# Expert loop of a mixture-of-experts layer: padding rows left out of the gathers, result rows stored by an indirect transfer

## The chip, the cores and the metric

The kernel runs on one core of one Trainium2 chip. The metric is the device time of one execution in microseconds (us); lower is better. The kernel before was run three times: 1900.81, 1901.49 and 1906.64 us, median 1901.49 us.

## What is computed

One inference step of a two-layer hybrid trunk for 640 tokens (128 context tokens and 512 latent tokens) of width 1024. Each layer has a mixer (three kinds of attention and a convolution, gated and summed) and then a mixture of experts, and only the latter matters here:

```python
lg = h @ moe_w_group + moe_b_group              # 4 groups
gi = argmax(lg);  gw = max(softmax(lg))
le = (h @ moe_w_expert + moe_b_expert)          # 16 experts, 4 per group
tv, ti = top_k(le[its group], 2)                # two experts per token
tw = softmax(tv) * gw
gate, up = split(h @ moe_w1[e])                 # 1024 -> 2 x 256
y += tw_e * (silu(gate) * up) @ moe_w2[e]       # 256 -> 1024
x = x + gate2 * y
```

640 tokens with two experts each make 1280 rows of work per layer. Counted with the reference on its drawn inputs, experts 0 to 15 get 97, 58, 88, 105, 82, 105, 144, 95, 59, 43, 50, 56, 64, 84, 71 and 79 rows in layer 0, and 50, 65, 63, 60, 63, 66, 46, 61, 113, 104, 86, 101, 74, 115, 103 and 110 in layer 1.

## The kernel before, in words

Everything is in fp32 in memory; a matmul is made of three fp16 passes (high times high, high times low, low times high; L428), so each weight tile that arrives is split: ScalarE writes the high part (L1617), VectorE subtracts to get the low part (L2363).

**Routing.** VectorE (L2391 to L2512) finds each token's two experts, and each row's place in a list of chunks. A chunk is 128 rows of one expert. Chunks 0 to 15 are the first 128 rows of experts 0 to 15; rows beyond 128 of an expert go to chunks from 16 on. Rows of an expert fill its chunk from row 0 up, one row per SBUF partition; what is left of the chunk is padding. `idxall` (one column per chunk, one entry per partition) holds the token number of each row, and 0 for padding, so a padding row is a copy of token 0. `sloti` holds, for each token, where its two result rows are. `route_ready` lets the loop start.

**The expert loop** runs over p*2+5 chunks; with these inputs p is 6 in both layers, which makes 17 chunks (c = 0 to 16) in each. Work per chunk:

- POOL (GpSimd, L1784 to L1789) waits until the transposes of chunk c-2 have left the buffer, copies the index column and issues an indirect DMA that gathers the 128 token rows (4 KB each) of chunk c from `h2_rows` in HBM into `xg[c % 2]`. The trace calls that tensor `h_rows`, and the buffer, which lies in a larger one, `hpart`. The first three chunks are gathered ahead of the loop (L1780 to L1782), chunk 0 into a buffer of its own.
- PE (TensorE, L1230 to L1249) computes in the order: gate/up matmuls of chunk c, k = 0 to 4 (15 matmuls), the 8 transposes of chunk c+1's rows (L1185, `turn_rows`, which counts `ht_done`), gate/up k = 5 to 7 (9 matmuls), the down matmuls of chunk c-1 (12), 2 transposes of the activations (L1208).
- ScalarE casts and copies (L1617, L1640, L1646, L1652) and copies the result out of PSUM into `ybuf[c % 2]` (L1659, `rows_back`, which counts `my_ready`); before that it waits until the store of chunk c-2 from the same buffer has landed (`y_out`, L1658).
- SP (SyncE) issues, in its own order, three 1 MB weight loads per chunk (L709: two halves of w1, and w2), each of which waits until the low part of the tile that it overwrites is made (L737, L739), and one store of 128 result rows to `y_rows` (512 KB, L745), which waits for `my_ready`. In the queue the store of a chunk stands ahead of the next weight loads.

All DMAs, whoever issues them, run on the same 16 DMA engines.

**After the loop** POOL waits until all stores have landed (L1792, L1793), copies the slot indices (L1794) and issues ten indirect gathers of result rows (L1799); ScalarE scales (L1697) and VectorE adds (L2568) them, PE turns them back (L1262), VectorE adds to x (L2577). In layer 0 VectorE first runs sixteen bias adds for the next layer (L1938).

`y_rows` was filled once with finite numbers in layer 0 (L617), long before the loop.

## Time and profile before

| | us |
|---|---|
| median of the three runs | 1901.49 |
| the profiled execution, its own time | 1910.62 |
| its span in the trace | 1908.8 |
| expert loop, layer 0 and layer 1, from the first to the last transposes | about 173 and 171 |

Busy over the span: PE 87%, VectorE 63%, ScalarE 47%, POOL 22%. The page of the profile gives busy times and groups of instructions; its other views give waits, the chain of work that ended last (each instruction followed back to what released it), a timeline of one engine, the DMA issues with their time from issue to landing, and busy times by stretch. "Idle before" is the time an engine sat still just before an instruction, with the instruction that ended it.

### The profile page before, as it was taken

Reading aid. Unit: us, or ns where it says so; the run is one execution under the profiler, and the core shown is the slowest. Engines: PE = TensorE matmul, PEld = TensorE weight load, DVE = VectorE, ACT = ScalarE, POOL = GpSimd, SP = SyncE. Lnnn points to the kernel's source line nnn. Section 1 sums busy time; section 2 is a strip of 40 time slices with the busy share of each in tenths; the row PEclk is TensorE's granted clock in tenths of the full one; section 3 lists DMA queues with packets and bytes.
Section 4 is the critical chain, followed back from the end, with each engine's and each line's share of the span. In section 5 each row is a group of like instructions: output and inputs, shape, how many; then the busy total and the mean of one; then the engine's idle time right before and its main releaser. Section 6 shows DMA issues by size and latency. Waiting matters only on the chain.

```text
span 1908.8 us, 34493 instructions
## 1 busy us (share of the span) xinstructions
PE 1657.5 (87%) x13277; PEld 1112.8 (58%) x13277; DVE 1198.3 (63%) x1900; ACT 893.7 (47%) x1468; POOL 425.7 (22%) x418
## 2 busy tenths in 40 slices
PE   6799889999989974888778998899999999388776
PEld 4478766777665542434455886677776556244336
DVE  4595455777537546877665925477773584787754
ACT  3322455666541123777533226466664211377653
POOL 0033243222241201212102324322222221111102
PEclk7899999999999986999859999999999999699995
DMA  8555235532327465999624732222223553399954
GB/s 296 181 197 171 68 132 182 183 104 73 115 104 255 157 253 190 350 380 365 241 112 144 246 125 87 77 98 73 73 73 127 197 195 120 126 362 371 373 210 166
DMA packets 191106, 350.71 MB, mean 184 GB/s; under 512 B 15477, under 2 KB 98934, under 8 KB 190710
## 3 DMA queue, kind: packets, MB, share of 16 engines
q1 hardware_dynamic: 181647, 319.58, 47.8%
q0 software_dynamic: 7776, 28.32, 4.0%
q8 instruction: 97, 1.59, 0.3%
q10 hardware_dynamic: 1543, 0.88, 0.2%
q14 instruction: 43, 0.35, 0.1%
HBM read 287.72 MB, written 61.01 MB: 183 GB/s over the span
## 4 chain that ended last, share of the span: by engine, by line
PE 65%; DVE 12%; DMA 9%; ACT 5%; issue 5%; DVEq 2%; SPq 1%; another core or an unknown queue 1%; ACTq 0%; POOL 0%; POOLq 0%
PE PS L431 38%; PE PS L438 10%; DMA wf<-in_moe_w 5%; PE PS L1055 3%; PE PS L1039 3%; DMA arena<-in_moe_w 3%; PE PS L857 2%; PE PS L813 1%; DVE arena L2363 1%; PE PS L839 1%; PE PS L823 1%; ACT arena L1439 1%; DVE hpart L1862 1%; DVE scratch L1853 1%; DMA wf<-in_w_out 1%
## 5 line engine op out<-in xcount | busy, mean ns | idle before, releaser
L1722 POOL TENSOR_TENSOR wlo<-wf,whi 128x256 f16<-128x256 f32 (+1 forms) x268 | 278.1, 1071 | 911.4 <-ACT whi L1366 911.4
L431 PE MATMUL PS<-hpart,whi 128*128 128x320 f16 x2048 | 426.5, 301 | 15.5 <-ACT arena L1439 14.5
L431 PE MATMUL PS<-hpart,wlo 128*128 128x320 f16 x1024 | 308.0, 301 | 0.0
L431 PE MATMUL PS<-whi,hpart 128*128 128x256 f16 (+2 forms) x1568 | 298.4, 291 | 5.9 <-DVE scratch L1983 3.6
L431 PEld LDWEIGHTS PS<-hpart,whi 128*128 128x128 f16 x2048 | 191.5, 98 | 104.4 <-issue 34.9
L431 PE MATMUL PS<-wlo,hpart 128*128 128x256 f16 (+2 forms) x784 | 225.7, 290 | 0.0
L431 PEld LDWEIGHTS PS<-whi,hpart 128*128 128x128 f16 x1568 | 151.9, 98 | 65.2 <-issue 24.1
L2363 DVE TENSOR_TENSOR arena<-arena 128x2048 f16<-128x2048 f32 x66 | 149.5, 2288 | 36.0 <-ACT arena L1617 35.8
L2159 DVE TENSOR_REDUCE stat<-PS 128x1 f32<-128x640 f32 (+1 forms) x160 | 110.7, 713 | 80.3 <-PE PS L1039 77.6
L1439 ACT ACTIVATE arena<-PS,pcol 128x320 f32<-128x320 f32 x128 | 67.4, 527 | 173.3 <-PE PS L431 167.9
L1617 ACT CAST arena<-arena 128x2048 f16<-128x2048 f32 x66 | 123.4, 1897 | 41.2 <-DMA arena<-in_moe_w 28.1
L1993 DVE SCALAR_TENSOR_TENSOR scratch<-scratch,cw 128x655 f32<-128x655 f32 x120 | 138.8, 1198 | 4.8 <-issue 0.4
L1529 ACT ACTIVATE scratch<-PS,stat 128x640 f32<-128x640 f32 (+1 forms) x160 | 112.9, 708 | 39.2 <-DVE stat L2159 38.3
L1366 ACT CAST whi<-wf 128x1024 f16<-128x1024 f32 (+1 forms) x84 | 109.8, 1307 | 39.7 <-PE PS L438 28.9
L431 PEld LDWEIGHTS PS<-hpart,wlo 128*128 128x128 f16 x1024 | 100.8, 98 | 40.1
L2144 DVE TENSOR_TENSOR arena<-PS,arena 128x640 f16<-128x640 f32 (+1 forms) x120 | 85.6, 713 | 49.1 <-ACT arena L1548 46.2
L2363 DVE TENSOR_TENSOR wlo<-wf,whi 128x2048 f16<-128x2048 f32 x36 | 82.3, 2291 | 43.1 <-ACT whi L1617 41.7
L431 PE MATMUL PS<-arena,hpart 128*128 128x512 f16 x384 | 96.3, 404 | 4.3 <-issue 4.1
L1548 ACT CAST arena<-PS 128x640 f16<-128x640 f32 (+1 forms) x120 | 72.8, 606 | 57.1 <-PE PS L1055 57.0
L1404 ACT COPY arena<-PS 128x256 f32<-128x256 f32 (+1 forms) x80 | 28.8, 360 | 145.0 <-PE PS L431 145.0
L431 PE MATMUL PS<-arena,scratch 128*128 128x512 f16 x408 | 93.6, 379 | 2.8 <-DVE scratch L2531 2.8
L438 PE MATMUL PS<-arena,whi 128*128 128x128 f16 (+1 forms) x512 | 91.2, 301 | 1.6 <-DVE arena L2280 1.6
(348 smaller groups left out, 2809.6 us busy)
## 6 DMA issues: line engine op xcount, KB each, us to landing
arena<-in_moe_w SPq DMA_DIRECT2D x66, 1024.0 KB, 9.9
arena<-in_w_ada SPq DMA_DIRECT2D x40, 1024.0 KB, 7.4
wf<-in_moe_w SPq DMA_DIRECT2D x36, 1024.0 KB, 9.8
wf<-in_w_gate SPq DMA_DIRECT2D x32, 1024.0 KB, 5.5
g_rows<-arena SPq DMA_DIRECT2D x128, 160.0 KB, 1.8
wf<-in_w_in SPq DMA_DIRECT2D x18, 1024.0 KB, 7.7
y_rows<-scratch SPq DMA_DIRECT2D x34, 512.0 KB, 8.8
arena<-g_rows SPq DMA_DIRECT2D x24, 640.0 KB, 5.1
```

The source lines that it names most:

```text
L431: ins = pe.matmul(out, st, mv, start=first and n == 0, stop=last and n == 2)
L438: ins = pe.matmul(pr(pair)[:, a:b], st, mv[:, a:b], start=first and n == 0, stop=last and n == 2)
L1366: return act.copy(whi[j][:, a:b] if dst is None else dst, wf[j][:, a:b])
L1439: act.activation(sg(n), bank(7, 320), ACT.Tanh, scale=0.5, bias=pcol[:, PC_BG + u % 4 * 8 + d:PC_BG + u % 4 * 8 + d + 1]).then_inc(g_ready ...
L1529: act.activation(ex[:, m % 4, 0:nk], pr(m % 2)[:, 0:nk], ACT.Exp, bias=stat[:, 0, m:m + 1], accum_out=stat[:, 1, m:m + 1]).then_inc(ex_rea ...
L1548: act.copy(pthi[:, hd % 2, 0:nk], pr(2)[:, 0:nk]).then_inc(pt_hi.sem, 1)
L1617: act.copy(mwhi[3 * j + q], mwf[3 * j + q]).then_inc(mw_hi.sem, 1)
L1722: ins = pool.tensor_tensor(lo[:, a:b], wf[j][:, a:b], hi[:, a:b], ALU.subtract)
L1993: ins = dve.scalar_tensor_tensor(out=zacc[:, c, :], in0=zpad[:, c, k:k + NZ], scalar=cw[:, c, k:k + 1], in1=zacc[:, c, :], op0=ALU.mult, o ...
L2144: dve.tensor_tensor(ptlo[:, hd % 2, 0:nk], pr(2)[:, 0:nk], pthi[:, hd % 2, 0:nk], ALU.subtract).then_inc(pt_ready.sem, 1)
L2159: dve.tensor_reduce(stat[:, 0, m:m + 1], pr(m % 2)[:, 0:nk], AX_X, ALU.max, negate=True).then_inc(mx_ready.sem, 1)
L2363: dve.tensor_tensor(mwlo[3 * j + q], mwf[3 * j + q], mwhi[3 * j + q], ALU.subtract).then_inc((mw_lo2 if q == 2 else mw_lo).sem, 1)
```

## The change

Three things are changed, all around the expert loop.

1. Padding entries of the index lists are made larger than the highest token number (except on partition 0, which stays a real token), and the gathers are told that an index beyond 639 is not transferred. The first three gathers keep indices within bounds, so that the buffers hold finite numbers. VectorE gets five small operations at the start of the routing and one more ahead of `route_ready`.
2. Result rows are no longer stored by SP but by an indirect DMA on POOL (`rows_to`), with a list `slotrow` that gives each partition its row in `y_rows`, or for padding a row beyond the bound, which is not transferred. It is made by two VectorE operations after `route_ready`. All stores leave SP's queue.
3. The order on POOL: the gather of chunk c now waits for the transposes of chunk c-1 (before: of chunk c-2), and the store of chunk c-4 is issued behind the gather of chunk c. The last four stores follow after the loop. Two tiny indirect loads at the start of the kernel take the place of the first counts of `y_out`.

```diff
--- before.py
+++ after.py
@@ -270,6 +270,7 @@
         rcol = wuf32[:, 300:340].rearrange("p (q t) -> p q t", t=5)
         ex5 = wuf32[:, 340:365].rearrange("p (t n) -> p t n", t=5)
         tie = sb("tie", [P, 4])
+        spared = sb("spared", [P, 8])
         small = wulo[:, :].bitcast(F32)
         rk = small[:, 0:266]
         iota, before = rk[:, 0:P], rk[:, P:2 * P]
@@ -279,6 +280,11 @@
         smalli = small[:, 276 + CHUNKS + 2:448].bitcast(I32)
         sloti, idxi = smalli[:, 0:10], smalli[:, 10:12]
         cexp = smalli[:, 12:12 + CHUNKS + 1]
+        idx3, slotrow = smalli[:, 38:41], smalli[:, 41:41 + CHUNKS + 2]
+        spare = small[:, 276 + CHUNKS + 2:448]
+        tokneg, padding, limit = spare[:, 68:73], spare[:, 73:74], spare[:, 74:75]
+        ownslot, padslot = spare[:, 75:75 + CHUNKS + 2], spare[:, 102:102 + CHUNKS + 2]
+        rowi = smalli[:, 129:131]
         loopf = sb("loopf", [P, 3])
         loopi = sb("loopi", [P, 3], I32)
         zero1 = sb("zero1", [P, 1], I32)
@@ -400,6 +406,7 @@
         rows_out = sig("rows_out", TILES * 16)
         route_in = sig("route_in", 16)
         route_ready = sig("route_ready", 1)
+        slots_ready = sig("slots_ready", 1)
 
         filled = sig("filled")
         base_ready = sig("base_ready", 1)
@@ -739,12 +746,6 @@
                         sp.wait_ge(mw_lo2.sem, past + (c - 1))
                     load(ds(e, 1), j, q)
 
-                def store(c, j, row):
-
-                    sp.wait_ge(my_ready.sem, past + (c + 2))
-                    sp.dma_start(t["y_rows"][ds(row, P), :] if not isinstance(row, int) else t["y_rows"][row:row + P, :],
-                                 ybuf[j]).then_inc(y_out[j].sem, 16)
-
                 sp.wait_ge(*filled(0, CHUNKS * 16))
                 load_next(2, 0, 0, 2)
                 for c in (1, 2):
@@ -757,20 +758,15 @@
                 with sp.Fori(1, p + 1) as i:
                     for n in range(2):
                         c, j = i * 2 + (1 + n), 1 - n
-                        store(i * 2 + (n - 2), n, i * (2 * P) + (n - 2) * P)
                         load_next(i * 2 + (2 + n), 1, n, i * 2 + (2 + n))
                         load_next(i * 2 + (2 + n), 2, n, i * 2 + (2 + n))
                         load_next(i * 2 + (3 + n), 0, j, i * 2 + (3 + n))
-                store(p * 2, 0, p * (2 * P))
                 load_next(p * 2 + 4, 1, 0, p * 2 + 4)
                 load_next(p * 2 + 4, 2, 0, p * 2 + 4)
-                store(p * 2 + 1, 1, p * (2 * P) + P)
                 if ahead:
                     sp.wait_ge(mw_lo.sem, past * 2 + (p * 4 + 10))
                     for u in range(2):
                         in_load(l + 1, u)
-                for c in range(3):
-                    store(p * 2 + (c + 2), c % 2, p * (2 * P) + (c + 2) * P)
                 if ahead:
                     late_load(l + 1)
 
@@ -1711,6 +1707,10 @@
 
         @block.gpsimd
         def _(pool):
+            pool.wait_ge(*set_ready(0, 5))
+            for j in range(2):
+                pool.indirect_dma_start(out=spared[:, 4 * j:4 * j + 4], out_offset=None, in_=t["k_tie"],
+                                        in_offset=bass.IndirectOffsetOnAxis(ap=zero1[:, :], axis=0)).then_inc(y_out[j].sem, 16)
             for l in range(LAYERS):
                 def low(count, j, dst=None, n=2048, piece=1024):
 
@@ -1767,7 +1767,25 @@
                 def rows_from(dst, index, done):
 
                     pool.indirect_dma_start(out=dst, out_offset=None, in_=t["h2_rows"],
-                                            in_offset=bass.IndirectOffsetOnAxis(ap=index, axis=0)).then_inc(done.sem, 16)
+                                            in_offset=bass.IndirectOffsetOnAxis(ap=index, axis=0),
+                                            bounds_check=TOK - 1, oob_is_err=False).then_inc(done.sem, 16)
+
+                def rows_to(c, j):
+
+                    pool.wait_ge(my_ready.sem, past + (c + 2))
+                    pool.tensor_tensor(rowi[:, j:j + 1], slotrow[:, ds(c, 1)], zero1[:, :], ALU.add)
+                    pool.drain()
+                    pool.indirect_dma_start(out=t["y_rows"],
+                                            out_offset=bass.IndirectOffsetOnAxis(ap=rowi[:, j:j + 1], axis=0),
+                                            in_=ybuf[j], in_offset=None,
+                                            bounds_check=CHUNKS * P - 1, oob_is_err=False).then_inc(y_out[j].sem, 16)
+
+                def rows_next(c, j):
+
+                    pool.wait_ge(ht_done.sem, past + (c - 1 + 1))
+                    pool.tensor_tensor(idxi[:, j:j + 1], idxall[:, ds(c, 1)], zero1[:, :], ALU.add)
+                    pool.drain()
+                    rows_from(xg[j], idxi[:, j:j + 1], xg_in[j])
 
                 pool.wait_ge(*rows_out(l, TILES * 16))
                 pool.tensor_tensor(zero1[:, :], zero1[:, :], zero1[:, :], ALU.add)
@@ -1777,16 +1795,21 @@
                 pool.wait_ge(*route_ready(l, 1))
                 pool.tensor_tensor(zero1[:, :], zero1[:, :], zero1[:, :], ALU.add)
                 pool.drain()
-                rows_from(xg0, idxall[:, 0:1], first_in)
-                rows_from(xg[1], idxall[:, 1:2], xg_in[1])
-                rows_from(xg[0], idxall[:, 2:3], xg_in[0])
+                rows_from(xg0, idx3[:, 0:1], first_in)
+                rows_from(xg[1], idx3[:, 1:2], xg_in[1])
+                rows_from(xg[0], idx3[:, 2:3], xg_in[0])
                 p = pairs_now(pool)
-                with pool.Fori(0, p + 1) as i:
+                pool.wait_ge(*slots_ready(l, 1))
+                pool.wait_ge(*filled(0, CHUNKS * 16))
+                rows_next(3, 1)
+                rows_next(4, 0)
+                rows_to(0, 0)
+                with pool.Fori(1, p + 1) as i:
                     for n in range(2):
-                        pool.wait_ge(ht_done.sem, past + (i * 2 + (2 + n)))
-                        pool.tensor_tensor(idxi[:, 1 - n:2 - n], idxall[:, ds(i * 2 + (3 + n), 1)], zero1[:, :], ALU.add)
-                        pool.drain()
-                        rows_from(xg[1 - n], idxi[:, 1 - n:2 - n], xg_in[1 - n])
+                        rows_next(i * 2 + (3 + n), 1 - n)
+                        rows_to(i * 2 + (n - 1), 1 - n)
+                for c in range(1, 5):
+                    rows_to(p * 2 + c, c % 2)
 
                 pool.wait_ge(hs_ready.sem, past + (p * 2 + 5))
                 pool.wait_ge(y_out[0].sem, b * 16 + (p * 16 + 64))
@@ -1813,8 +1836,6 @@
             for s in (w_lo, wo_lo, pt_ready, ot_ready, mgu_done, msilu_ready, mact_ready, at_done, at_hi, at_ready,
                       my_done, my_ready):
                 dve.nop().then_inc(s.sem, 1)
-            for s in y_out:
-                dve.nop().then_inc(s.sem, 16)
             dve.nop().then_inc(comb_ready.sem, TILES)
             dve.nop().then_inc(m_used.sem, 2)
             dve.nop().then_inc(x1_ready.sem, 2)
@@ -2388,6 +2409,13 @@
                     dve.tensor_tensor(out, out, col(7, T4), ALU.is_equal)
                     dve.drain()
 
+                dve.wait_ge(*route_in(l, 16))
+                dve.tensor_scalar(tokneg, tokid, -1024.0, None, ALU.add)
+                dve.tensor_scalar(padding, tokid[:, 0:1], 1.0, 4096.0, ALU.min, ALU.mult)
+                dve.tensor_scalar(ownslot, iota[:, 0:CHUNKS + 2], float(P), None, ALU.mult)
+                dve.drain()
+                dve.tensor_scalar(limit, padding, float(TOK - 1 - 1024), None, ALU.add)
+                dve.tensor_scalar(ownslot, ownslot, tokid[:, 0:1], None, ALU.add)
                 lg = route[:, :, 0:4]
                 oh, oh1, oh2, sel, sel2 = (rw[:, :, 16 + 4 * q:20 + 4 * q] for q in range(5))
                 first_max(lg, oh, 0)
@@ -2484,7 +2512,7 @@
                 dve.drain()
                 for ch in range(2):
                     half = chhot[:, 5 * ch:5 * ch + 5, :]
-                    ins = dve.tensor_tensor(half, half, bc(tokid.rearrange("p (n o) -> p n o", o=1), [P, 5, CH]), ALU.mult)
+                    ins = dve.tensor_tensor(half, half, bc(tokneg.rearrange("p (n o) -> p n o", o=1), [P, 5, CH]), ALU.mult)
                 ins.then_inc(place_ready.sem, 1)
                 for tile in range(3, TILES):
                     row_tile(tile)
@@ -2496,7 +2524,13 @@
                 count(loopf[:, 1:2], incl[:, 15:16], iota[:, 1:CHUNKS + 1:2], ALU.is_gt, 1, PAIRS + 1)
                 dve.tensor_scalar(loopi[:, 1:2], loopf[:, 1:2], -2.0, None, ALU.add)
                 dve.wait_ge(*list_done(l, 1))
-                dve.tensor_copy(idxall, bank(5, CHUNKS + 2)).then_inc(route_ready.sem, 1)
+                found = bank(5, CHUNKS + 2)
+                dve.tensor_scalar(idx3, found[:, 0:3], 1024.0, float(TOK - 1), ALU.add, ALU.min)
+                dve.tensor_scalar(idxall, found, limit, 1024.0, ALU.min, ALU.add).then_inc(route_ready.sem, 1)
+                dve.scalar_tensor_tensor(out=padslot, in0=found, scalar=0.0, in1=bc(padding, [P, CHUNKS + 2]),
+                                         op0=ALU.is_equal, op1=ALU.mult)
+                dve.drain()
+                dve.tensor_tensor(slotrow, padslot, ownslot, ALU.add).then_inc(slots_ready.sem, 1)
                 dve.wait_ge(*rexp_ready(l, 1))
 
                 dve.tensor_reduce(rcol[:, 3, :], ex5[:, :, 0:4], AX_X, ALU.add)
```

## Rows read from the trace of the kernel before

**Rows 1.** Busy times of two stretches, the expert loops of layers 0 and 1.

```profile
core 0: us, PE busy (x) PEld busy (x) DVE busy (x) ACT busy (x) POOL busy (x), PEclk, DMA share, GB/s
752.00:918.00 166.00, 141.68 (x683) 69.45 (x684) 130.07 (x91) 119.49 (x104) 35.66 (x28) 0.95 0.97 356
1668.00:1833.00 165.00, 141.35 (x685) 69.89 (x684) 127.60 (x90) 117.34 (x102) 29.14 (x28) 0.96 1.00 364
```

**Rows 2.** The chain that ended last, 793 to 840 us: start us, us, what.

```profile
805.33 12.91 DMA arena<-in_moe_w
...
839.01 0.37 SPq L745
```

**Rows 3.** Waits of SP's queue, 752 to 918 us: engine, line, waited for, total, times, longest.

```profile
SPq L709 <- DVE arena L2363: 91.7, 16, 11.6
SPq L745 <- ACT scratch L1659: 13.3, 9, 2.7
```

**Rows 4.** POOL by form, 752 to 918 us: line, operation, xcount, busy us, mean ns, idle before.

```profile
L1769 POOL DMA_INDIRECT hpart<-h_rows,wulo x14 | 25.6, 1832 | 17.9 <-issue 17.9
L1787 POOL TENSOR_TENSOR wulo<-wulo,zero 128x1 int32<-128x1 int32 x14 | 10.0, 715 | 105.8 <-PE PS L1185 105.8
```

**Rows 5.** Gathers of 770 to 920 us, issue to landing.

```profile
DMA to landing us min/median/max: 6.9/8.3/9.4
```

**Rows 6.** Timeline of PE around the transposes of chunks 2, 4 and 16, layer 0.

```profile
763.74 1.04 PE L1185 MATMUL PS<-ident,hpart 128*128 128x128 f32 x8
...
782.63 1.04 PE L1185 MATMUL PS<-ident,hpart 128*128 128x128 f32 x8
783.50 2.10 PE L431 MATMUL PS<-arena,hpart 128*128 128x512 f16 x9
785.44 2.75 PE L431 MATMUL PS<-arena,scratch 128*128 128x512 f16 x12
...
921.02 1.04 PE L1185 MATMUL PS<-ident,hpart 128*128 128x128 f32 x8
```

**Rows 7.** Timeline of PE, the transposes of chunks 2 and 16, layer 1.

```profile
1679.39 1.04 PE L1185 MATMUL PS<-ident,hpart 128*128 128x128 f32 x8
...
1834.64 1.04 PE L1185 MATMUL PS<-ident,hpart 128*128 128x128 f32 x8
```

**Rows 8.** Timeline of POOL at the transposes of chunk 2.

```profile
764.96 0.32 POOL L1787 TENSOR_TENSOR wulo<-wulo,zero 128x1 int32<-128x1 int32 x1 [5.73 <-PE PS L1185]
766.12 2.14 POOL L1769 DMA_INDIRECT hpart<-h_rows,wulo  x1 [0.84 <-issue]
```

**Rows 9.** VectorE's part of the routing, layer 1.

```profile
1634.04 0.18 DVE L2382 TENSOR_TENSOR wuhi<-wuhi 128x20 f32<-128x20 f32 x1
1634.30 0.18 DVE L2384 TENSOR_TENSOR wuhi<-wuhi,tie 128x20 f32<-128x20 f32 x1
```

**Rows 10.** The chain that ended last, end of the loop in layer 1.

```profile
1855.41 1.02 ACT scratch L1659
...
1856.60 2.59 DMA y_rows<-scratch
...
1860.47 0.95 POOL arena L1799
...
1861.73 5.15 DMA hpart<-y_rows,wulo
```

**Rows 11.** Timeline of VectorE after the loop in layer 0.

```profile
958.58 1.26 DVE L1938 TENSOR_TENSOR bias<-PS,arena 64x448 f32<-64x448 f32 x2 [5.87 <-remote]
...
960.34 1.28 DVE L2568 SCALAR_TENSOR_TENSOR scratch<-hpart,wuhi,arena 128x1024 f32<-128x1024 f32 x1
```

**Rows 12.** Gathers of result rows after both loops, issue to landing.

```profile
DMA to landing us min/median/max: 6.2/6.4/6.5
```

**Rows 13.** Two gathers issued at 1661.07 and 1663.24 us: the DMA issues, us to landing.

```profile
hpart<-h_rows,wulo POOLq DMA_INDIRECT x1, 8.1
...
hpart<-h_rows,wulo POOLq DMA_INDIRECT x1, 9.8
```

## The prediction

> **What bounds the kernel now.** I read the busy times of the two expert loops first [rows 1]: the 16 DMA engines are busy 0.97 and 1.00 of the time, PE 142 of 166 us. Then the timeline of PE: from the transposes of chunk 2 to those of chunk 16 it takes 921.02 - 763.74 = 157.3 us in layer 0 [rows 6] and 1834.64 - 1679.39 = 155.3 us in layer 1 [rows 7]. That is 14 chunks, so 11.23 and 11.09 us per chunk, mean 11.16. Per chunk of 11.16 us PE works 141.68/166 x 11.16 = 9.5 us, VectorE 8.7 and ScalarE 8.0 [rows 1]. So the loop is bound by the DMA engines: a chunk moves 3 MB of weights, 0.5 MB of gathered rows and 0.5 MB of result rows. The chain of waits agrees: a weight load of 12.91 us stands in it, issued behind a store in SP's queue [rows 2]. SP itself waits for buffers to come free, 91.7 us, and only 13.3 us for results [rows 3], so its queue is a small matter while the engines are full.
>
> **What is saved at most.** 17 chunks x 128 = 2176 rows are moved each way per layer, 1280 of them real: 41% are padding. Rows are 1 of 4 MB of a chunk, so 0.41 x 0.25 = 10.3% of the loop's bytes go. If all of that reached the DMA engines' time, the cycle would be 11.16 x 0.897 = 10.0 us, and PE's 9.5 us plus the stops of its in-order queue are then next. I take 10.3 us as the floor of the cycle.
>
> **The gather becomes a round trip.** The gather of chunk c was issued after the transposes of chunk c-2, and had two cycles to land. Now it is issued after the transposes of chunk c-1 and is needed by the next ones, one cycle later; PE's queue is in order, so behind those transposes stand 9 gate/up matmuls, the down matmuls and the next chunk. The cycle can't be shorter than this loop:
> - the transposes, 1.04 us [rows 6];
> - until POOL's copy starts, 764.96 - 764.78 = 0.18 us [rows 6, 8];
> - copy, drain and start of the indirect DMA: (10.0 + 17.9)/14 = 1.99 us on average [rows 4];
> - issue to landing: 6.9, 8.3 and 9.4 us (least, median, most) [rows 5].
>
> With 8.3 us that is 11.5 us, above today's 11.16; with 6.9 us it is 10.1. Today this costs nothing, since two cycles (22 us) cover it. The first intervals of the loop are shorter than the mean, (782.63 - 763.74)/2 = 9.4 us [rows 6], and those are stretched as well. How much does a gather gain from moving 41% fewer rows? Lower bound of the gain 0. Upper bound: it lands in 6.9 us, the best of today. In the quiet stretch after the loops, with DMA engines not full, full gathers still took 6.2 to 6.5 us [rows 12], so most of the time isn't the rows. Leaving out 41% of the load-dependent part, 0.41 x (8.3 - 6.3) = 0.8 us, is the most that I can argue from rows, and half of that, 0.4, is nearest to both; I take 7.9 us. Cycle: 1.04 + 0.18 + 1.99 + 7.9 = 11.1 us. 14 cycles = 155.5 us: -1.8 us in layer 0 and +0.2 in layer 1, **-1.6 us**; the bounds are 161.1 us each (+9.6 in sum) and 144.2 us each at the floor of 10.3 (-24.2).
>
> **Stores on POOL.** 34 stores leave SP, whose loads could then be issued earlier; while the DMA engines are full, that only makes them queue longer: nothing, and up to the 13.3 us of waiting per layer [rows 3] should they stand idle, which the 0.97 and 1.00 speak against. POOL gets a second copy and indirect DMA per chunk: 2 x (0.72 + 1.28 + 1.83) = 7.7 us [rows 4], below the cycle, so POOL's queue holds. Is a result buffer free in time? The store of chunk c is issued behind the gather of chunk c+4, so from the start of the transposes of chunk c+3: 1.04 + 0.18 + 1.99 + 1.83 + 1.99 = 7.0 us, and lands 8.3 us later at 15.3. The copy into the same buffer waits for the down matmuls of chunk c+2, whose end is a cycle plus the stretch from 782.63 to 788.19 [rows 6] later: 11.1 + 5.6 = 16.7 us. 1.4 us to spare; its price is nothing while that holds. What is queued behind the store on POOL is the next gather, some 7 us away.
>
> **Head of the loop.** Five small VectorE operations ahead of the first maximum, with two dependent steps of 0.26 us [rows 9] and some 0.05 to 0.1 for each of the others, and one more ahead of `route_ready`: 0.7 us per layer, **+1.4 us**. The two behind `route_ready` delay only low parts of weights. The wait for the index of the stores and for the fill of `y_rows` ended long before.
>
> **Tail.** In layer 1 the chain runs copy to `ybuf`, store, gathers [rows 10]: the copy ends at 1856.43, the store lands 2.59 us after its issue at 1856.60. The indirect store needs about 1.16 us until its issue (764.96 to 766.12) [rows 8] and then lands in 2.6 us (as SP's did) at least, in 6.5 [rows 12] at most; I take the 5.15 us after which the first pair of indirect gathers released ScalarE [rows 10]. 1.2 + 5.15 - 2.8 = +3.5, less a little since the last chunk of layer 1 is empty but for one row: **+3.2 us** (+1.0 to +4.9). In layer 0 VectorE reaches the sums only at 960.34, behind bias adds that stood still 5.87 us until 958.58 [rows 11]. What they wait for ("remote") isn't shown; it may move with the gathers or not: 0 to 3.2, **+1.6 us**.
>
> **Sum.** -1.6 + 1.4 + 3.2 + 1.6 = +4.6 us on the profiled execution of 1910.6 us, which stands 9 us above the median; so 1906.1 against 1901.5.
>
> **One rule weighed.** The DMA engines' share is a mean over 16 [rows 1], which doesn't show whether relief is even. The Trainium skill, "DMA: Bandwidth & Descriptors", section "The descriptor swizzle", says that in a 128-partition transfer each engine serves fixed partitions: engines 0 to 7 partitions 0 to 63, the others 64 to 127. By it a sum would lack the DMA relief almost wholly (rival B). No row here shows it.
>
> **Rivals.**
> - A. *The relief reaches the loop.* Gathers land in 7 us or less and the cycle falls to 10.3 us. For it: full DMA engines [rows 1] and 10.3% fewer bytes, the store's wait gone from SP. Against: 8.3 us of landing of which 6.3 remain in quiet [rows 5, 12]. -24.2 + 6.2 = -18.0: **1883.5 us**.
> - B. *Slower: the gather lands no sooner.* Padding sits at the high rows of a chunk. If a row's partition fixes its DMA engine, the half of the engines with rows 0 to 63 keeps, by the counts per expert, 986 and 983 of 1088 rows (9% less), the other half 294 and 297 (73% less). A weight load and a gather land with the slowest engine. So the landing stays 8.3 us, the cycle is 11.5: +9.6 + 6.2 = +15.8, **1917.3 us**. It decides from a landing of 8.0 us on, where the round trip passes today's cycle.
> - C. *Two indirect DMAs per chunk hold each other up.* At the start of layer 1, the third of three gathers issued close together landed in 9.8 us and the second in 8.1 [rows 13]. Were every one 9.8, the cycle would be 13.0: 182 us per loop, +52 + 6: **1960 us**. Against: gather and store are issued some 4 us apart and the next gather 7 us later.
> - D. *Rows beyond the bound are moved or cost as much all the same*: then B's time.
>
> **Chances.** Forecast (round trip near 11.1 us, between 10.9 and 11.4) 0.45; A 0.27; B and D 0.22; C 0.06. The measurement can tell about 0.3%, 5.7 us, from no change. The forecast's own range is 1901 to 1914: of its 0.45, 0.04 are faster, 0.23 within and 0.18 slower. B has 0.02 within. Faster 0.31, same 0.25, slower 0.44. Likeliest time 1906 us. The range reaches from A (1883) past B, 1883 to 1922; C is left out. Cases of both signs hold most of the chance, and the forecast lies close to the border of "no change".
>
> **What would show it.** Right: PE waits before the transposes (L1185) for the gather in most chunks, the interval from chunk 2's to chunk 16's stays near 155 us, DMA share falls to about 0.9, SP's wait for results is gone, the end of layer 1 is 3 us longer from the last copy to the first gather. Wrong: intervals of 145 us with gathers landing in 7 us (A); a DMA share near 0.9 with landings of 8 us and more and intervals above 160 (B); landings of 10 us (C); as many software packets as before plus those of the stores (D); ScalarE waiting for `y_out` at its copy.

## The result and the profile after

Eight executions, four of each kernel: 1992.99 us for the changed kernel (1987.28 to 2001.80) against 1901.29 us for the kernel before (1900.81 to 1906.64). The ratio is 1.048, with an interval of 1.0437 to 1.0523. It is slower by 92 us, where 1906 was forecast and 1922 was the end of the range. Of the runs of the experiments one (2509.77 us, of e5_count_for_drain) showed a granted clock of 0.64 where its other seven had 0.92 to 0.93, and its ratio leaves it out.

The profiled execution of the changed kernel took 1992.42 us with a span of 1990.6, that of before 1910.62 with 1908.8. The stretches of the two loops that answer to [rows 1], with the busy times of the engines in the same columns, granted clock, DMA share and GB/s last:

```profile
790.00:950.00 160.00, 116.31 (x484) 57.50 (x482) 92.95 (x63) 86.66 (x75) 32.20 (x42) 0.84 0.74 260
1720.00:1880.00 160.00, 119.13 (x504) 59.49 (x503) 98.45 (x68) 88.72 (x77) 32.93 (x42) 0.85 0.75 257
```

The DMA engines have fallen from 0.97 and 1.00 to 0.74 and 0.75, and no engine is fuller than before. PE works 116 of 160 us. So the loop is bound by a wait and not by work. Its pace, from the transposes of chunks 2 and 16 of each layer (timeline of PE, answers to [rows 6, 7]):

```profile
764.63 0.93 PE L1181 MATMUL PS<-ident,hpart 128*128 128x128 f32 x7
...
963.66 1.09 PE L1181 MATMUL PS<-ident,hpart 128*128 128x128 f32 x8 [1.58 <-DMA hpart<-h_rows,wulo]
...
1717.65 1.04 PE L1181 MATMUL PS<-ident,hpart 128*128 128x128 f32 x8
...
1918.41 1.09 PE L1181 MATMUL PS<-ident,hpart 128*128 128x128 f32 x8 [0.73 <-DMA hpart<-h_rows,wulo]
```

That is 199.0 us in layer 0 (157.3 before) and 200.8 in layer 1 (155.3 before): +41.8 and +45.5, 87.3 us in all. The rest of the kernel is 5.5 us shorter (+0.9 ahead of chunk 2 of layer 0, -4.4 between the loops, -2.0 behind the second), which gives the +81.8 us between the two profiled executions. The whole loss is in the loops. Within them a chunk takes 15.0 us over most of the way, for example from 831.63 to 846.56.

What the engines wait for, from 790 to 950 us (time in all, times, longest):

```profile
POOL hpart L1769 <- issue: 76.6, 11, 7.2
POOL y_rows L1778 <- issue: 48.3, 10, 5.3
...
PE PS L1181 <- DMA hpart<-h_rows,wulo: 41.4, 10, 7.0
...
POOL wulo L1786 <- PE PS L1181: 0.2, 1, 0.2
```

PE waits 4 us per chunk for the gathered rows (L1181). POOL waits 7.0 us ahead of each gather and 4.8 ahead of each store, 125 of 160 us, and nothing that the profile can name ends these waits ("issue"). For PE it almost never waits (0.2 us in all). So POOL, 20% busy, sets the pace. Its timeline over one chunk and a half:

```profile
826.24 1.01 POOL L1769 DMA_INDIRECT hpart<-h_rows,wulo  x1 [7.05 <-issue]
827.28 0.20 POOL L1776 TENSOR_TENSOR wulo<-wulo,zero 128x1 int32<-128x1 int32 x1
832.46 1.46 POOL L1778 DMA_INDIRECT y_rows<-scratch,wulo  x1 [4.98 <-issue]
833.95 0.20 POOL L1786 TENSOR_TENSOR wulo<-wulo,zero 128x1 int32<-128x1 int32 x1
841.24 1.01 POOL L1769 DMA_INDIRECT hpart<-h_rows,wulo  x1 [7.10 <-issue]
```

From gather to store 6.22 us, from store to the next gather 8.78: 15.0 together. Between the copy of the index, 0.2 us long, and the indirect DMA stands only the drain. The instructions of its sequencer show it (L1777 ahead of the store, L1787 ahead of the gather; shortest, median and longest in ns, 790 to 950 us), and in the second fence the one drain per chunk of the kernel before, in its loop:

```profile
L1777 POOLq DRAIN  x11: 5197/5486/6138, 796.3 to 945.8; - x11
L1787 POOLq DRAIN  x11: 5984/6805/8392, 787.1 to 938.5; - x11
```

```profile
L1788 POOLq DRAIN  x10: 345/1428/3174, 798.4 to 897.4; - x10
```

And the landings of the indirect DMAs in that stretch (median us behind their issue):

```profile
hpart<-h_rows,wulo POOLq DMA_INDIRECT x11, 5.4
y_rows<-scratch,wulo POOLq DMA_INDIRECT x10, 7.9
```

The drain behind a gather takes 5.5 us where gathers land in 5.4. The drain behind a store takes 6.8 where stores land in 7.9 and the drain begins about 1.2 us after the issue. One by one it fits too. In the chain of waits POOL's first instruction behind the drain starts at 831.69 and at 840.50; the gather of 826.24 landed 5.3 us later, at 831.5, the store of 832.46 7.9 us later, at 840.4. The same holds for each of the 20 drains from 802 to 952 us: its record ends 0.1 us behind the landing of the indirect DMA ahead of it.

The padding rows do stay out: the packets of the indirect queue moved 32.91 MB, where all rows moved both ways make 46.15 MB (e4_all_rows below).

```profile
q0 software_dynamic: 12736, 32.91, 4.5%
```

### The profile page after: what moved, and what is told of

It is laid out like the page before. It is cut to its first block, busy times and chain, and to the rows that moved or that the text cites. A ratio compares the mean times of both kernels' runs of the same rounds, so it can differ in the third digit from the quotient of the medians.

```text
span 1990.6 us, 34617 instructions
## 1 busy us (share of the span) xinstructions
PE 1692.0 (85%) x13277; PEld 1131.2 (57%) x13277; DVE 1207.3 (61%) x1916; ACT 893.3 (45%) x1468; POOL 464.9 (23%) x488
## 3 DMA queue, kind: packets, MB, share of 16 engines
q0 software_dynamic: 12736, 32.91, 4.5%
## 4 chain that ended last, share of the span: by engine, by line
PE 56%; issue 21%; DVE 8%; DMA 7%; ACT 3%; POOL 2%; POOLq 2%; DVEq 1%; SPq 0%; ACTq 0%
PE PS L438 33%; PE PS L445 8%; DMA hpart<-h_rows,wulo 4%; PE PS L1051 3%; PE PS L1035 3%; PE PS L853 2%; PE PS L809 1%; DMA wf<-in_w_out 1%; POOL hpart L1769 1%; PE PS L1181 1%; PE PS L835 1%; POOLq L1787 1%; ACT arena L1435 1%; DVE hpart L1883 1%; DVE scratch L1874 1%
## 5 line engine op out<-in xcount | busy, mean ns | idle before, releaser
L438 PE MATMUL PS<-whi,hpart 128*128 128x256 f16 (+2 forms) x1568 | 307.6, 297 | 5.9 <-DVE scratch L2004 3.6
L438 PE MATMUL PS<-wlo,hpart 128*128 128x256 f16 (+2 forms) x784 | 230.6, 297 | 0.0
L1181 PE MATMUL PS<-ident,hpart 128*128 128x128 f32 x272 | 52.1, 354 | 98.9 <-DMA hpart<-h_rows,wulo 98.9
L1362 ACT CAST whi<-wf 128x1024 f16<-128x1024 f32 (+1 forms) x84 | 109.8, 1307 | 39.8 <-DMA wf<-in_w_out 20.7
L1181 PEld LDWEIGHTS PS<-ident,hpart 128*128 128x128 f32 x272 | 41.5, 181 | 114.4 <-DMA hpart<-h_rows,wulo 113.5
L438 PE MATMUL PS<-arena,hpart 128*128 128x512 f16 x384 | 102.7, 424 | 0.3
```

Of the source, the lines that this page charges most:

```text
L438: ins = pe.matmul(out, st, mv, start=first and n == 0, stop=last and n == 2)
L1181: ins = pe.transpose(PS[:, 0, k * P:(k + 1) * P], rows[:, k * P:(k + 1) * P], ident[:, :])
L1362: return act.copy(whi[j][:, a:b] if dst is None else dst, wf[j][:, a:b])
```

## The experiments

**Theory** after this reading: the drain between the copied index and the indirect DMA stands until the indirect DMA ahead of it has landed; with two per chunk, a chunk takes two landings. **Rivals**: the indirect stores are slow whatever stands between; VectorE or a shared port holds POOL; the padding rows beyond the bound cost the time; the gather issued a cycle later costs it. The labels below are those of the kernels. Each ratio is taken against runs of the kernel before from the same batch, whose medians were 1907.20 us (experiments 1 to 3), 1894.22 (4 to 6) and 1905.40 (7 and 8), so ratios are to be compared and not times.

**1. Stores back on SP.** Both kernels keep the gathers with the bound; the stores are SP's plain ones of all 128 rows. The second also issues each gather a cycle earlier, as before.

```
 SP:    store(c, j, row) as in the kernel before, at the same places in its queue
 POOL:  - rows_to(...)                                              # both
 POOL:  - pool.wait_ge(ht_done.sem, past + (c - 1 + 1))             # second
        + pool.wait_ge(ht_done.sem, past + (c - 1))
```

> The stores go back to SP's queue as before; the gathers keep their bound and their late wait (transposes of chunk c-1). Theory 1 (POOL's queue: behind an indirect DMA, the next copy's drain stands until that DMA's descriptors are made, 6.2 us after a gather and 8.8 us after a store, 15.0 us per chunk in sum): with one indirect DMA per chunk POOL has time, the loop goes back to 11 us per chunk, total 1895 to 1920 us. Theory 2 (the late gather's round trip is what binds): stays within 30 us of 1993.

> As e1, and the gather of chunk c waits for the transposes of chunk c-2 again, as before; what is left of the change is the padding omitted from the gathers (5% of the loop's bytes) and six VectorE operations. Theory 1: 1885 to 1905 us. Against e1 it gives the price of the late wait where POOL is free: by my round trip (1.0 + 0.2 + 2.0 + landing of 5.4 to 8.3) 0 to 15 us. If DMA relief doesn't reach the slowest engine: 1900 to 1905 us.

Measured: 1913.49 us and 1902.97 us; ratios 1.0026 (0.9998 to 1.0053) and 0.9978 (0.9958 to 0.9999). With the stores off POOL the 90 us are gone. The late wait alone costs 10.5 us, the difference of the two medians (9 us by the ratios): in e1_sp_stores PE waited for the gathered rows 16.3 us in 160, in e2_sp_stores_early not at all. POOL's wait ahead of the gather is 1 us in both. The waits of e1_sp_stores, 790 to 950 us:

```profile
PE PS L1192 <- DMA hpart<-h_rows,wulo: 16.3, 11, 2.8
...
POOL hpart L1776 <- issue: 10.7, 12, 0.9
```

So the late gather is real, and a ninth of the loss in size. What is left of the change in the second kernel, above all the padding omitted from the gathers, is worth 0.2%.

**2. The padding rows moved as well.** The change with one constant different, so that padding indices stay valid.

```
-dve.tensor_scalar(padding, tokid[:, 0:1], 1.0, 4096.0, ALU.min, ALU.mult)
+dve.tensor_scalar(padding, tokid[:, 0:1], 1.0, 0.0, ALU.min, ALU.mult)
```

> The changed kernel with padding set to 0: every index is within bounds, so all 2176 rows are gathered and stored, through the same instructions. Theory 1 (making of descriptors and drain): POOL's cycle stays about 15 us or grows a little, total 1985 to 2020 us, with the DMA share up from 0.74 to about 0.85. Theory 3 (the omission itself makes the indirect DMA slow): the gaps of 5 and 7 us shrink, total below 1950 us.

Measured: 2006.14 us, ratio 1.0523 (1.0462 to 1.0584). The stops of POOL (its waits), the landings and, in the list of queues, 13 MB more:

```profile
POOL hpart L1769 <- issue: 78.2, 11, 7.4
POOL y_rows L1778 <- issue: 49.6, 10, 5.3
```

```profile
hpart<-h_rows,wulo POOLq DMA_INDIRECT x11, 5.5
y_rows<-scratch,wulo POOLq DMA_INDIRECT x10, 7.9
```

```profile
q0 software_dynamic: 12736, 46.15, 6.0%
```

A gather of all 128 rows lands in 5.5 us, one with the padding left out in 5.4; the store in 7.9 both times. The omission isn't the cause, and leaving out 41% of the rows is no help to a landing. Only where nearly all rows are left out does the landing shorten: the last gather of layer 1, one real row of 128, landed in 2.5 us in the changed kernel and in 5.1 with all rows, its store in 2.1 and 3.3; the last gather of layer 0, with 16 real rows, in 3.4 and 4.2.

**3. A count in place of the drain.** The copy of the index raises a semaphore, POOL waits for that count, and one more small operation stands between it and the indirect DMA.

```
-pool.tensor_tensor(idxi[:, j:j + 1], idxall[:, ds(c, 1)], zero1[:, :], ALU.add)
-pool.drain()
+pool.tensor_tensor(idxi[:, j:j + 1], idxall[:, ds(c, 1)], zero1[:, :], ALU.add).then_inc(copied.sem, 1)
+pool.wait_ge(copied.sem, past * 2 + (nth + 3))
+pool.tensor_tensor(smalli[:, 132:133], zero1[:, :], zero1[:, :], ALU.add)
```

The same with `rowi`, ahead of the store.

> The changed kernel, but the two index copies inside the loop are waited for by a count and not by a drain. Theory 1: the drain is what waits for the descriptors, so the gaps of 5 and 7 us ahead of the indirect DMAs go, and the loop comes down to 11 to 12 us per chunk, total 1900 to 1935 us. Theory 4 (descriptors are made one DMA after another at 6 to 8 us each, whatever the instructions do): the gaps go but landings grow to 10 us and more, and the total stays above 1970 us.

Measured: 1909.76 us, ratio 1.0013 (0.9982 to 1.0045). The order of the work, the number of indirect DMAs and their rows are those of the change. The drains of the loops are gone, with a count and a small operation in their place, and with them 83 us (89 by the ratios). Its waits, 790 to 950 us:

```profile
PE PS L1182 <- DMA hpart<-h_rows,wulo: 18.5, 9, 3.5
...
POOL y_rows L1781 <- issue: 7.8, 16, 0.5
POOL hpart L1770 <- issue: 4.7, 9, 0.5
```

POOL now stands 0.5 us ahead of each. This rules out that the indirect stores are slow as such. What is left is the late gather: PE waits 18.5 us in 160.

**4. One drain for both.** Both indices are copied, one drain, then gather and store behind each other.

```
+pool.tensor_tensor(idxi[:, j:j + 1], idxall[:, ds(c, 1)], zero1[:, :], ALU.add)
+pool.tensor_tensor(rowi[:, j:j + 1], slotrow[:, ds(c - 4, 1)], zero1[:, :], ALU.add)
+pool.drain()
+rows_from(xg[j], idxi[:, j:j + 1], xg_in[j])
+pool.indirect_dma_start(out=t["y_rows"], ...)
```

> The changed kernel with both index copies of a loop step under one drain, and gather and store issued one right behind the other. Theory 1 (a drain stands until the descriptors of the indirect DMAs before it are made, 5 to 7 us each): the drain now comes only in the next step and part of the work is done while POOL waits for PE. If gather and store need 6.2 + 8.8 us one after the other whatever stands between them, the cycle stays 15 us and the total 1990; if most of that was waiting without need, as the run with counts suggests (11.3 us per chunk), it falls to 11 to 13 us, total 1905 to 1950 us.

Measured: 1943.63 us, ratio 1.0247 (1.0201 to 1.0293), a cycle of 12.4 us. Half of the loss is gone with half of the drains. The two indirect DMAs go out 1.32 us apart (821.44 and 822.76). There is one drain per chunk, and it comes only when PE has freed the buffer (its records in ns, 790 to 950 us):

```profile
L1814 POOLq DRAIN  x12: 457/1526/7065, 791.0 to 931.7; - x12
```

Six of the twelve take 0.5 us, five 2.6 to 3.2 (there one of the two index copies itself takes 2.2 us) and one 7.1. So from the second chunk on it hardly waits for a landing, and the rest of the loss is another: POOL waits for PE (75.6 of 160 us), PE for the gather (27.8), and the round trip of the late gather is longer than in experiment 1. From the transposes at 816.56 it runs over the copies at 817.97 and the issue at 821.44, lands 9.0 us later beside a store in flight, and lets the next transposes start at 830.51, 13.95 us in all.

**5. Early gathers, with counts and with drains.** The wait of experiment 1 in the kernel of experiment 3, and in the change itself.

> Counts in place of the drains, and the gather of chunk c waits for the transposes of chunk c-2 as in the kernel before. In the run with counts and late gathers PE waited 0.9 to 3.5 us in most chunks for the gather, DMA share 0.94. If the round trip was the bound there, those waits go and the cycle comes down from 11.3 to 10.3 to 10.8 us: total 1880 to 1900 us, 0.4 to 1.2% faster than the kernel before. If DMA relief doesn't reach the slowest engine: cycle 11.1, total 1900 to 1910 us.

> The changed kernel with its drains, but gathers early (transposes of chunk c-2). Theory 1: POOL never waits for PE in the loop, so nothing changes, 1980 to 2000 us. Theory 2 (late gather): the loop falls by 2 us per chunk or more, total below 1940 us.

Measured: with counts 1897.40 us, ratio 1.0009 (0.9988 to 1.0029), so PE's waits for the gather go and the 0.4 to 1.2% expected of it don't come; with drains 1980.13 us, ratio 1.044 (1.0393 to 1.0486). With drains it matters little how early POOL may start, since its own queue is what is late (waits of e7_early_drain, 790 to 950 us):

```profile
POOL hpart L1769 <- issue: 69.1, 10, 7.2
POOL y_rows L1778 <- issue: 55.0, 11, 6.6
```

**6. Less for VectorE.** A rival was that POOL's drain stands because VectorE holds something that both use. The change with the low parts of w1 made for 256 of 2048 columns (`n` is 256 for the two tiles of w1 in the loop, 2048 elsewhere); the rest of them isn't computed.

```
-dve.tensor_tensor(mwlo[3 * j + q], mwf[3 * j + q], mwhi[3 * j + q], ALU.subtract
+dve.tensor_tensor(mwlo[3 * j + q][:, 0:n], mwf[3 * j + q][:, 0:n], mwhi[3 * j + q][:, 0:n], ALU.subtract
```

> The changed kernel, but inside the loop VectorE makes the low parts of the two w1 tiles of a chunk for 256 of 2048 columns only (the other columns keep old low parts), so that VectorE works 4 us less per chunk. If making descriptors is slowed by VectorE's work on the same memory: the gap ahead of the indirect DMA behind a store falls from 7 us towards 4, behind a gather from 5 towards 3, cycle 10 to 13 us. If descriptor making has its own pace: gaps stay 7 and 5 us and the cycle 15 us.

Measured, one execution: 1980.80 us. VectorE (third busy time) works 38 us in 110, where it was 63 in the change, and POOL stands as long:

```profile
790.00:900.00 110.00, 82.07 (x345) 40.60 (x343) 38.25 (x47) 61.77 (x54) 19.68 (x30) 0.86 0.79 274
```

```profile
POOL hpart L1769 <- issue: 70.5, 11, 7.2
POOL y_rows L1778 <- issue: 58.9, 11, 7.7
```

That rival falls.

**7. Landing or a fixed time?** The kernel before, with nothing of the change but a small operation and a drain directly behind each gather of its loop.

```
 rows_from(xg[1 - n], idxi[:, 1 - n:2 - n], xg_in[1 - n])
+pool.tensor_tensor(smalli[:, 132:133], zero1[:, :], zero1[:, :], ALU.add)
+pool.drain()
```

> The kernel before with one more small POOL operation and a drain directly behind each gather of the loop; nothing else of the change is in it. POOL has nothing to do there until the next gather, so no time is expected from it in either theory (within 5 us of before). Theory 1 (a drain stands until the indirect DMA ahead of it has landed): POOL's next instruction after that drain starts within 0.2 us of the gather's landing, 6.9 to 9.4 us behind its issue, varying with it. Theory 2 (the drain waits for something of POOL itself, such as the making of the descriptors, a fixed time): the next instruction stands at one fixed distance behind the issue, whether the gather lands in 7 or in 9 us.

Measured, one execution: 1901.67 us, beside 1905.4 for the kernel before (17 runs): the drain costs nothing where POOL has nothing to do. Four such drains in a row, each with its own length in ns, and under it the landing of the gather ahead of it (issued at 820.37, 830.04, 842.53 and 852.58):

```profile
L1791 POOLq DRAIN  x1: 7647/7647/7647, 820.2 to 820.2; - x1
...
L1791 POOLq DRAIN  x1: 9379/9379/9379, 829.9 to 829.9; - x1
...
L1791 POOLq DRAIN  x1: 7662/7662/7662, 842.3 to 842.3; - x1
...
L1791 POOLq DRAIN  x1: 8944/8944/8944, 852.4 to 852.4; - x1
```

```profile
hpart<-h_rows,wulo POOLq DMA_INDIRECT x1, 7.4
...
hpart<-h_rows,wulo POOLq DMA_INDIRECT x1, 9.1
...
hpart<-h_rows,wulo POOLq DMA_INDIRECT x1, 7.4
...
hpart<-h_rows,wulo POOLq DMA_INDIRECT x1, 8.7
```

The drains end at 827.8, 839.3, 850.0 and 861.3; the gathers landed at 827.8, 839.1, 849.9 and 861.3. The drain follows the landing to 0.2 us, at 7.4 us as at 9.1, so it isn't a fixed time of POOL's. The making of the descriptors doesn't take so long either: without a drain between, indirect DMAs go out 1.26 us apart [rows 10].

**8. What the omission is worth when POOL is out of the way.** The kernel of experiment 5 with counts, and with all rows moved as in experiment 2.

> The kernel of e6 (counts in place of the drains, early gathers) with the padding indices left at a valid row, so that all 128 rows of every chunk are moved each way: 10.3% more bytes in the loop than e6, nothing else changed. Theory 1 (with POOL out of the way the omission is what makes e6's cycle 10.56 and 10.77 us against 11.16 of before): the cycle goes back to 11.1 to 11.3 us in both layers, the time is 10 to 17 us above e6, that is 1.005 to 1.010 of the kernel before. Theory 2 (the shorter cycle of e6 comes from the loads that no longer stand behind stores in SP's queue, and the omitted rows give little, as in e2): the cycle stays within 0.15 us of e6's, the time within 4 us of it.

Measured: 1900.50 us, ratio 0.9979 (0.9950 to 1.0009), beside e6_count_early's 1.0009 (0.9988 to 1.0029). From the transposes of chunk 2 to those of chunk 16 it takes 149.1 and 147.8 us with all rows, 147.0 and 149.2 without the padding. The same stretch of both (DMA share and GB/s are the last two), all rows first:

```profile
790.00:900.00 110.00, 96.70 (x471) 47.67 (x472) 88.21 (x63) 83.53 (x73) 68.78 (x61) 0.97 1.02 387
```

```profile
790.00:900.00 110.00, 94.86 (x465) 47.17 (x466) 87.75 (x63) 82.72 (x72) 68.75 (x61) 0.97 0.95 349
```

With 10% fewer bytes the DMA engines are less full (0.95 against 1.02, 349 against 387 GB/s) and the chunks come no faster. Theory 2 of this experiment holds for the omission. That the freed queue of SP made the cycle shorter isn't shown: experiment 7's kernel, which has before's queues, takes 152.3 and 149.1 us, and e2_sp_stores_early 150.3 and 149.1, against 157.3 and 155.3 in the profiled execution of before. So a good part of what looks like a shorter cycle is the difference between one execution and another, which in before's runs of this batch went from 1894 to 1916 us. No variant is clearly faster than the kernel before; the lowest ratios are 0.9978 and 0.9979.

## Why the prediction was wrong

**The step that failed** is, in the part on the stores: "POOL gets a second copy and indirect DMA per chunk: 2 x (0.72 + 1.28 + 1.83) = 7.7 us [rows 4], below the cycle, so POOL's queue holds". The 1.28 us between copy and indirect DMA were taken as a fixed price of the drain. They were a mean over drains that already waited for landings. In the kernel before this gap runs from 0.82 to 2.80 us:

```profile
835.85 0.95 POOL L1769 DMA_INDIRECT hpart<-h_rows,wulo  x1 [0.82 <-issue]
842.21 1.05 POOL L1787 TENSOR_TENSOR wulo<-wulo,zero 128x1 int32<-128x1 int32 x1 [5.41 <-PE PS L1185]
846.05 0.95 POOL L1769 DMA_INDIRECT hpart<-h_rows,wulo  x1 [2.80 <-issue]
...
854.64 2.49 POOL L1769 DMA_INDIRECT hpart<-h_rows,wulo  x1 [2.26 <-issue]
864.75 0.19 POOL L1787 TENSOR_TENSOR wulo<-wulo,zero 128x1 int32<-128x1 int32 x1 [7.63 <-PE PS L1185]
865.77 2.14 POOL L1769 DMA_INDIRECT hpart<-h_rows,wulo  x1 [0.83 <-issue]
```

The gather of 835.85 landed after 9.4 us, at 845.3, behind the next copy: gap 2.80. The gather of 854.64 landed after 8.3 us, at 862.9, ahead of the next copy: gap 0.83. All 28 drains of the two loops go by this. 19 of them began with a gather in flight, and each ended within 0.3 us behind the landing or behind the end of the copy, whichever was later. A gather was issued every 11.2 us on average and landed in 8.3 [rows 5], so only the end of a landing was met, and the longest drain took 3.2 us. In the changed kernel the next drain comes right behind each indirect DMA and stands for its whole landing. The two terms of 3.83 us measured 6.2 and 8.8 us, the sum 15.0 in place of 7.7 (profile after), and above the 11.2 us of a cycle before. 14 cycles x (15.0 - 11.2) x 2 layers = 106 us at most; 87.3 were measured, since the first two intervals of each loop (10.3 and 10.9 us in layer 0), with gathers still in store, and the last (12.2) were shorter.

**The result buffer** was said to be free 1.4 us early, while POOL's queue holds. With POOL late it wasn't, which is one of the signs of being wrong on record: ScalarE waited for the landing of a store before its copy (790 to 950 us).

```profile
ACT scratch L1655 <- DMA y_rows<-scratch,wulo: 16.9, 9, 4.4
```

**The cycle of the gather's round trip** was right as a mechanism and in size, once POOL isn't in the way: 11.1 us was forecast, 155.5 us from chunk 2 to chunk 16. With the stores on SP (e1_sp_stores) PE waits for the gather in most chunks, and this stretch takes 155.1 and 155.8 us. Without the drains (experiment 3) it takes 158.2 and 151.9 us, and the ratio of 1.0013 (0.9982 to 1.0045) has the forecast's 1906.1/1901.5 = 1.0024 within. Part of this is luck. The landing of 7.9 us was a choice halfway between two bounds (e1_sp_stores has 7.8, e2_sp_stores_early with the same omission 8.3), and one bound was misread: the 6.2 to 6.5 us [rows 12] aren't those of a quiet stretch, since the ten gathers there go out 1.26 us apart and are in flight together. A full gather that was issued with no other indirect DMA in flight landed in 4.4 us (the first of the changed kernel, at 737.13).

**The head** was forecast at +0.7 us per layer; chunk 2 of layer 0 comes 0.9 us later. That doesn't measure it: in the nine other kernels with the operations of this routing it comes between 761.8 and 767.4 us, where it is 763.74 before and 764.63 after.

**The tail** of layer 1 was too dear. In layer 1 from the last copy to the first gather of results it takes 1942.75 - 1937.10 = 5.65 us, before 1860.47 - 1855.41 = 5.06 [rows 10]: +0.6 where 3.2 was forecast. The last store is issued at 1939.38, and POOL has its landing at 1941.69:

```profile
1939.38 0.99 POOL L1778 DMA_INDIRECT y_rows<-scratch,wulo  x1 [0.90 <-issue]
1941.69 0.20 POOL L1817 TENSOR_TENSOR wulo<-wulo,zero 128x10 int32<-128x10 int32 x1 [1.33 <-DMA y_rows<-scratch,wulo]
```

The 5.15 us taken for this landing were those of full gathers; this store has one row and landed in 2.1. In layer 0 the term even has the other sign. From the last copy (939.23 before, 981.92 after) to the first sum it takes 997.47 - 981.92 = 15.55 us, before 960.34 - 939.23 = 21.11: -5.6 where +1.6 was forecast, and about what the stretch between the loops got shorter (4.4). The bias adds that stood still before [rows 11] now run through, all 16 in one go, and the sums wait for the gathers:

```profile
982.70 10.27 DVE L1959 TENSOR_TENSOR bias<-PS,arena 64x448 f32<-64x448 f32 x16 [0.82 <-PE PS L874]
...
997.47 1.28 DVE L2602 SCALAR_TENSOR_TENSOR scratch<-hpart,wuhi,arena 128x1024 f32<-128x1024 f32 x1 [4.07 <-ACT arena L1693]
```

Before, loads for the next layer stood behind the last three stores in SP's queue, and now nothing stands there. All four kernels with the stores on SP have two stops of 3.7 to 6.0 us in the bias adds, and the eight with the stores on POOL have none. That it is these loads that the adds waited for is likely and not shown.

**Rival C** foresaw that two indirect DMAs per chunk hold each other up, and its 1960 us with a chance of 0.06 is the nearest of all. That nearness is luck, as it had the wrong mechanism: it wanted landings of 9.8 us, and they were 5.4 and 7.9. Its "against", that the two are issued 4 us apart, was itself built on the failed step.

**Rival A**, the relief of the DMA engines, doesn't come even where nothing is in its way: 0.9978 (0.9958 to 0.9999) with half of it (experiment 1), and no difference between all rows and real rows alone (experiment 8). The prediction read a DMA share of 0.97 and 1.00 as the bound of the loop; 10% fewer bytes lower the share and leave the time. Which chain keeps the chunk at 10.5 us then wasn't settled. In e6_count_early it runs over weight loads (41%), stretches that no wait explains (20.7%), VectorE (9.8%) and PE (9.5%).

**Rival B** had one thing right: a gather without its padding lands no sooner, 5.4 us against 5.5 (experiment 2). Whether this is because a row's partition fixes its DMA engine, as the Trainium skill says in "DMA: Bandwidth & Descriptors", section "The descriptor swizzle", isn't shown, as the records here don't name the DMA engine. It would fit: by that rule a chunk with 43 real rows still gives some engines their full share, and its gather landed in 5.3 us; with 16 real rows no engine has more than half of it, and the gather landed in 3.4. In this change it decided nothing.

**Rival D** is half right. Rows beyond the bound aren't moved (32.91 MB, where all rows make 46.15), but they save no time in a usual chunk (experiments 2 and 8). Its sign, the number of packets, was badly chosen: it is 12736 with and without the omission.

## What to carry to other kernels

Price a drain by what will be in flight when it comes, not by its mean in another order of work: on POOL a drain behind an indirect DMA is a wait for that DMA's landing. Where POOL issues more than one indirect DMA per step, wait for the count of the copy that made the index (1.0013 in place of 1.048 here). And a full DMA share is no proof that bytes are the bound: e9_count_early_all and e6_count_early move 387 and 349 GB/s (790 to 900 us) at the same pace.

## What the runs showed of the hardware

- POOL's drain stands until the indirect DMA ahead of it has landed, for gathers (7.4 to 9.1 us, experiment 7) as for stores (6.8 us behind landings of 7.9, its end 0.1 us behind the landing). In the kernel before its length was 0.35 to 3.2 us, by how much of the landing, or of the index copy just ahead (0.2 to 2.1 us), was left. The profile doesn't name a releaser for it: the wait is put down to "issue" of the next indirect DMA, and is found by the DRAIN records of the sequencer.
- Without a drain, indirect DMAs of 128 rows of 4 KB go out 1.26 us apart [rows 10], and several are in flight at once.
- Leaving 41% of the rows out of a gather didn't shorten its landing (5.4 against 5.5 us), nor that of the store (7.9 both). Leaving out 127 of 128 did (2.5 against 5.1 us, and 2.1 against 3.3 for the store).
- Gathers landed in 5.4 us with the DMA engines at 0.74, and in 8.3 us with them at 0.97 [rows 1, 5]; a full one, issued with no other indirect DMA in flight, landed in 4.4.
- In the kernels with counts POOL stood 3.6 us at the drain ahead of the gathers of results, where the change stood 0.9. That costs them 2.7 us per layer, and nothing here explains it.
